# A two-layer fp32 trunk on one core: residual update moved into the next normalisation loop, half of its products on GpSimd, and four smaller reorderings

## The chip, the core and the metric

The kernel runs on one core of a Trainium2 chip. Its engines are TensorE (PE in the profile, its weight loads PEld), VectorE (DVE), ScalarE (ACT), GpSimd (POOL) and SyncE (SP, whose queue issues most of the DMAs). The metric is the device time of one execution in microseconds.

## The reference

Two layers of a diffusion trunk work on 640 tokens (128 context, 512 latent). Each layer is two sandwich-normalised sub-layers with modulation:

```python
h = rmsnorm(x, pre_mix_g) * (1 + sc1) + sh1
x = x + g1 * rmsnorm(token_mixing(h), post_mix_g)
h = rmsnorm(x, pre_ffn_g) * (1 + sc2) + sh2
up = depthwise_conv(h @ ffn_up)                 # 3 taps, 2 x 2816 columns
x = x + g2 * rmsnorm((silu(gate) * val) @ ffn_down, post_ffn_g)
# sh, sc, g = split(silu(c) @ ada_w + ada_b), for each layer and token group
```

Token mixing is one wide input projection, four branches (attention, a depthwise convolution, gated spatial mixing, pooling), sigmoid gates, a merge and an output projection.

## The kernel before

Activations lie with features on the 128 partitions and 644 token columns (640 and halo) along the free axis, in chunks of 128 features: x, yb (the sub-layer's output with its gain, not yet divided by its rms) and h have 8 chunks, the feed-forward `act` 22. Every product is fp32 made of three passes: both operands are split in a high and a low part, and PE runs high*high, high*low (activations) and low*high (weights). Weight blocks of 128x512 come by DMAs of SP's queue into 4 slots; POOL splits each into `w_hi` (L470) and `w_lo` (L472), PE uses them, ACT copies results out of PSUM, DVE does most of the elementwise work. PSUM is used as 4 sets of two banks; counting semaphores `set_full`, `set_empty`, `w_split`, `w_used` pass them round. Each engine runs its own program, a loop over the two layers, so the order on each engine is the order in which the code is written.

A layer's stages: head (`next_mod`, `next_h`: the first h), p1 (input projection), the branches, merge, out, gap2 (`output_norms`, then x is updated and h is made again), up, down, and tail (`output_norms`, x is updated). What the change touches:

- `update_x(c)` (L1401, L1403): yb = yb * inv_rms, x = x + yb, two DVE instructions of 128x644 for each chunk. In gap2 three updates stand ahead of `next_h` and five within it; in tail all eight stand at the end of the layer's loop body.
- `next_h` (L1423, L1433): for each chunk DVE makes `hx` = x * scale * inverse rms, ACT rounds `h_hi`, DVE makes `h_lo`. PE's first group of a stage starts when h_lo of chunk 0 is there.
- At the start of a layer SP requests two rounds of p1's weights, waits on `layer_free`, and requests `par` (gains and biases) and `tables`. POOL waits on the same semaphore, clears `conv_x` and splits weights. In the first layer ACT gives `layer_free` after the head's modulation.
- up: 11 steps of 4 sets; a half step of two sets is called an item here (items 0 to 21; item 2i + q is half q of step i). For an item PE runs two products of 8 feature chunks, ACT copies the two sets into `up_x` (L1234), DVE runs the three taps (L1793, L1798), ACT a tanh, DVE the gate (L1805, L1808). The two sets of an item come free for item + 2 when ACT has copied them. Meanwhile DVE sums "trios" of modulation columns over chunks (`ada`: L1377 twice, L1379 14 times, 128x384); PE adds each trio over partitions with 6 one-column matmuls (L572) ahead of a product, and waits for the trio there.
- down: 2 passes over the 22 chunks of `act`, a chunk is 24 matmuls over all 4 sets; ACT and DVE make the high and low part of a chunk (`hi_part` L1255, `lo_part` L1815) before PE needs it. Between the passes ACT evacuates the 4 sets (`outputs`), and DVE's `add_square`, `cross` and `add_products` (L1307, L1360, L1365, L1367) add up the statistics of the first four output chunks. Chunks are numbered on through both passes, 0 to 43.

## Time and profile before

| | us |
|---|---|
| median of 3 runs | 2651.12 (2649.63 to 2651.96) |
| profiled execution, its own time | 2648.95 |
| its span from the first to the last instruction | 2647.1 |
| PE busy | 2404.7 (91%) |
| DVE busy | 1807.2 (68%) |
| POOL busy | 1332.7 (50%) |
| ACT busy | 555.8 (21%) |

The profile is one execution. Busy shares are averages over stages that wait for different engines, so what one edit is worth is read from the stretch that it touches. In the timeline a row gives the start, the duration, the engine, the line, the operation with its tiles, the count of merged instructions and, in brackets, how long the engine stood idle before and what ended that.

### The profile page before, as it was taken

Reading aid. Unit: us, or ns where it says so; the run is one execution under the profiler, and the core shown is the slowest. Engines: PE = TensorE matmul, PEld = TensorE weight load, DVE = VectorE, ACT = ScalarE, POOL = GpSimd, SP = SyncE. Lnnn points to the kernel's source line nnn. Section 1 sums busy time; section 2 is a strip of 40 time slices with the busy share of each in tenths; the row PEclk is TensorE's granted clock in tenths of the full one; section 3 lists DMA queues with packets and bytes.
Section 4 is the critical chain, followed back from the end, with each engine's and each line's share of the span. In section 5 each row is a group of like instructions: output and inputs, shape, how many; then the busy total and the mean of one; then the engine's idle time right before and its main releaser. Section 6 shows DMA issues by size and latency. Waiting matters only on the chain.

```text
span 2647.1 us, 44389 instructions
## 1 busy us (share of the span) xinstructions
PE 2404.7 (91%) x14854; PEld 2228.2 (84%) x14854; DVE 1807.2 (68%) x2357; ACT 555.8 (21%) x989; POOL 1332.7 (50%) x1240
## 2 busy tenths in 40 slices
PE   5897989999997999999959888899999799999996
PEld 5894548999986999999959744699999689999986
DVE  5558765554489898976573786555436888989566
ACT  1203442111121111123211144410111211111232
POOL 2458314555553656565435761065555445656551
PEclk9998999999997999999969989899999799999997
DMA  5210002333321323322212101033332223323221
...
DMA packets 100491, 212.04 MB, mean 80 GB/s; under 512 B 10208, under 2 KB 17824, under 8 KB 100384
## 3 DMA queue, kind: packets, MB, share of 16 engines
...
q8 instruction: 59, 0.97, 0.2%
q14 instruction: 48, 0.39, 0.1%
...
## 4 chain that ended last, share of the span: by engine, by line
PE 55%; DVE 17%; DVEq 16%; issue 6%; ACT 5%; POOLq 1%; DMA 1%; ACTq 0%; POOL 0%; SPq 0%
PE ps L539 31%; PE ps L883 9%; DVEq L1795 4%; PE ps L559 4%; DVEq L1382 3%; PE ps L755 3%; DVE ada_part L1379 3%; DVEq L1801 3%; DVE up_y L1793 2%; PE ps L701 2%; DVE x L1403 1%; PE ps L572 1%; ACT up_x L1234 1%; DVE yb L1401 1%; PE ps L744 1%
## 5 line engine op out<-in xcount | busy, mean ns | idle before, releaser
L470 POOL TENSOR_SCALAR w_hi<-w_raw 128x512 fp32r<-128x512 f32 x552 | 378.7, 686 | 1107.9 <-PE ps L539 237.5
L472 POOL TENSOR_TENSOR w_lo<-w_raw,w_hi 128x512 fp32r<-128x512 f32 x552 | 769.8, 1395 | 81.4 <-issue 1.4
L539 PE MATMUL ps<-h_hi,w_hi 128*128 128x322 f32 x2688 | 627.5, 315 | 5.3 <-POOL w_lo L472 5.3
L539 PE MATMUL ps<-h_lo,w_hi 128*128 128x322 f32 x2688 | 623.6, 313 | 0.0
L539 PE MATMUL ps<-h_hi,w_lo 128*128 128x322 f32 x2688 | 620.3, 312 | 0.0
L539 PEld LDWEIGHTS ps<-h_hi,w_hi 128*128 128x128 f32 x2688 | 455.5, 191 | 8.7 <-POOL w_lo L472 7.4
L539 PEld LDWEIGHTS ps<-h_lo,w_hi 128*128 128x128 f32 x2688 | 458.2, 191 | 0.0
L539 PEld LDWEIGHTS ps<-h_hi,w_lo 128*128 128x128 f32 x2688 | 458.2, 191 | 0.0
L1379 DVE SCALAR_TENSOR_TENSOR ada_part<-ada_raw,cond,ada_part 128x384 f32<-128x384 f32 x448 | 342.2, 805 | 17.1
L1798 DVE SCALAR_TENSOR_TENSOR up_y<-up_x,par,up_y 128x644 f32<-128x644 f32 x176 | 216.0, 1267 | 13.9 <-issue 12.7
L1815 DVE TENSOR_TENSOR a_lo<-act,a_hi 128x644 fp32r<-128x644 f32 x84 | 130.0, 1549 | 116.1 <-ACT a_hi L1255 113.7
L883 PE MATMUL ps<-a_hi,w_hi 128*128 128x322 f32 x640 | 150.7, 317 | 19.8 <-DVE a_lo L1815 16.3
L1735 DVE SCALAR_TENSOR_TENSOR mtmp<-gate_t,ps 128x644 f32<-128x644 f32 x48 | 39.4, 821 | 173.1 <-ACT gate_t L1181 131.7
L883 PE MATMUL ps<-a_hi,w_lo 128*128 128x322 f32 x640 | 149.5, 316 | 0.0
L883 PE MATMUL ps<-a_lo,w_hi 128*128 128x322 f32 x640 | 149.3, 315 | 0.0
L1241 ACT ACTIVATE up_t<-up_y 128x644 f32<-128x644 f32 x44 | 32.7, 743 | 473.3 <-DVE up_y L1798 473.3
L883 PEld LDWEIGHTS ps<-a_hi,w_hi 128*128 128x128 f32 x640 | 109.0, 193 | 25.2 <-DVE a_lo L1815 18.2
L1181 ACT ACTIVATE gate_t<-ps,half_gate 128x644 f32<-128x644 f32 x64 | 51.2, 800 | 341.0 <-PE ps L539 337.5
L559 PE MATMUL ps<-h_hi,w_hi 128*128 128x322 f32 x256 | 63.5, 331 | 58.5 <-DVE h_lo L1433 58.5
L507 POOL TENSOR_TENSOR conv_acc<-conv_acc,conv_tmp 128x655 f32<-128x655 f32 x60 | 105.9, 1765 | 8.8 <-issue 0.2
L883 PEld LDWEIGHTS ps<-a_hi,w_lo 128*128 128x128 f32 x640 | 109.9, 193 | 0.0
L883 PEld LDWEIGHTS ps<-a_lo,w_hi 128*128 128x128 f32 x640 | 109.6, 193 | 0.0
...
## 6 DMA issues: line engine op xcount, KB each, us to landing
...
```

What stands on the lines that cost most here:

```text
L470: pool.tensor_scalar(w_hi[:, s, 0:n * P], raw, 1.0, 0.0, ALU.mult, ALU.add)
L472: pool.tensor_tensor(w_lo[:, s, 0:n * P], raw, w_hi[:, s, 0:n * P], ALU.subtract).then_inc(w_split[s], 1)
L507: pool.tensor_tensor(conv_acc[:, 0, 0:CLEN], conv_acc[:, 0, 0:CLEN], dst, ALU.add)
L539: last = pe.matmul(ps[:, 2 * s + j, 0:HALF], w, a[:, j * HALF:(j + 1) * HALF], start=(k == 0 and i == 0), stop=(k == total - 1 and i == 2))
L559: last = pe.matmul(ps[:, 2 * s + j, 0:HALF], w, a[:, j * HALF:(j + 1) * HALF], start=(k == 0 and i == 0), stop=(k == DC - 1 and i == 2))
L755: pe.matmul(ps[0:V_HEAD, 7, :], v_pair[:, b, vs], probs_t[:, b, :], start=(b == 0), stop=(b == 4))
L883: last = pe.matmul(ps[:, 2 * s + j, 0:HALF], w, a[:, j * HALF:(j + 1) * HALF], start=(start and i == 0), stop=(stop and i == 2))
L1379: last = dv.scalar_tensor_tensor(out=acc[:, g, 0:n, :], in0=w, scalar=cond[:, k, g:g + 1], in1=acc[:, g, 0:n, :], op0=ALU.mult, op1=ALU.add)
L1382: dv.drain()
L1795: dv.drain()
L1798: last = dv.scalar_tensor_tensor(out=up_y[:, j, :], in0=up_x[:, j, 1 + tap:1 + tap + TOK], scalar=col("ffn_dw", v, tap), in1=up_y[:, j, :] ...
L1815: dv.tensor_tensor(a_part_of(n, False), src, a_part_of(n, True), ALU.subtract).then_inc(a_ready, 1)
```

## The change

Five edits come together.

1. x is updated within the `next_h` that follows. `next_h` first updates chunks 0 and 1, then chunk c + 2 inside its loop, at every call: in gap2, and at the head of a layer, where it now does the update that stood at the end of the layer before (for the first layer with zeros in yb and in the inverse rms, which are cleared at the start). The last layer's update stands after the loop. POOL multiplies chunks 4 to 7 by the inverse rms (`scale_outputs`, after it has split the stage's first round of weights), and DVE only adds those.
2. `ada_pre` and `ada_pre_part` lie at other addresses, and x is requested after the second part of `ada_pre` instead of the third.
3. `par` is requested ahead of p1's weights on a semaphore of its own, `tables` after p1's first round; `layer_free` is given at the start for the first layer; POOL neither waits for it nor clears `conv_x`, which DVE does after `next_h`.
4. Middle of down: the last two chunks of the first pass run set by set (`last_chunks`), and chunks 22 and 23 have buffers of their own, so that ACT and DVE make their parts ahead of the evacuation; each later `lo_part` stands one place earlier among the statistics.
5. up: the trios after the first stand before DVE's items 4, 7, 10, 13, 16, 19 instead of 3, 6, 9, 12, 15, 18, and PE uses them at the second product of items 2, 8, 14 and 20 and at the first of items 6, 12 and 18, instead of at the first product of items 2, 5, 8, 11, 14, 17 and 20.

```diff
+POOL_SCALES = range(DC // 2, DC)
@@ SP
-            sp.wait_ge(ada_pre_loaded[2], 16)
+            sp.wait_ge(ada_pre_loaded[1], 16)
...
-                load_linear(L, "p1", 0, 2)
+                sp.wait_ge(par_free, L + 1)
+                sp.dma_start(par[:, :], params_in[bass.ds(L, 1)].rearrange("a p n -> (a p) n")).then_inc(par_loaded, 16)
+                load_linear(L, "p1", 0, 1)
                 sp.wait_ge(layer_free, L + 1)
-                sp.dma_start(par[:, :], params_in[bass.ds(L, 1)].rearrange("a p n -> (a p) n")).then_inc(par_loaded, 16)
...
+                load_linear(L, "p1", 1, 1)
@@ POOL
+            def scale_outputs(n_inv):
+
+                pool.wait_ge(inv_ready, n_inv)
+                for c in POOL_SCALES:
+                    pool.tensor_tensor(yb[:, c, :], yb[:, c, :], inv_rms[:, :], ALU.mult).then_inc(yb_scaled, 1)
...
-                pool.wait_ge(layer_free, L + 1)
-                pool.sem_inc(pool_steps, 1)
-                pool.memset(conv_x[:, :, :], 0.0).then_inc(halo_zero, 1)
-                split_linear(L, "p1", P1_BLOCKS // SLOTS)
+                split_linear(L, "p1", 1)
+                scale_outputs(L * NINV + 1)
+                split_linear(L, "p1", P1_BLOCKS // SLOTS, 1)
...
-                split_linear(L, "up", UP_BLOCKS // SLOTS)
+                split_linear(L, "up", 1)
+                scale_outputs(L * NINV + 3)
+                split_linear(L, "up", UP_BLOCKS // SLOTS, 1)
@@ PE, up
-                    up_step(r * 3 + 1, late_trio(L, 2) + r * 2, 0)
-                    up_step(r * 3 + 2, late_trio(L, 3) + r * 2, 2)
-                    up_step(r * 3 + 3)
-                up_step(10, late_trio(L, 8), 0)
+                    up_step(r * 3 + 1, late_trio(L, 2) + r * 2, 1)
+                    up_step(r * 3 + 2)
+                    up_step(r * 3 + 3, late_trio(L, 3) + r * 2, 0)
+                up_step(10, late_trio(L, 8), 1)
@@ PE, down
+                def last_chunks(q, first):
+                    end = (q + 1) * FFC - 1
+                    for s in range(4):
+                        for n in range(first, end + 1):
...
-                        for k in range(LAST4, FFC):
-                            down_chunk(q, c0 + k, (c0 + k) // SLOTS, (c0 + k) % SLOTS, k % 2, False, k == FFC - 1)
...
+                        for k in (LAST4, LAST4 + 1):
+                            down_chunk(q, k, k // SLOTS, k % SLOTS, k, False, False)
+                        last_chunks(0, LAST4 + 2)
@@ ACT, down
                 hi_part(FFC, 0)
+                hi_part(FFC + 1, 1)
                 ac.wait_ge(gain_ready, 2 * L + 2)
                 outputs(0)
-                hi_part(FFC + 1, 1)
                 for k in range(2, 2 + SLOTS):
+                    hi_part(FFC + k, k)
                     square_of_scaled(k - 2, down_sq2, L * 2 * DC + DC + k - 2)
-                    hi_part(FFC + k, k)
@@ DVE
-            def update_x(c):
-
-                dv.tensor_tensor(yb[:, c, :], yb[:, c, :], inv_rms[:, :], ALU.mult)
-                dv.drain()
+            def update_x(c, n_scaled):
+
+                if c in POOL_SCALES:
+                    dv.wait_ge(yb_scaled, n_scaled + c - POOL_SCALES[0] + 1)
+                else:
+                    dv.tensor_tensor(yb[:, c, :], yb[:, c, :], inv_rms[:, :], ALU.mult)
+                    dv.drain()
                 return dv.tensor_tensor(x[:, c, :], x[:, c, :], yb[:, c, :], ALU.add)
...
+                dv.wait_ge(inv_ready, n_inv - 1)
+                update_x(0, n_scaled)
+                dv.drain()
+                update_x(1, n_scaled)
+                dv.drain()
                 dv.wait_ge(inv_ready, n_inv)
...
-                    if c + 1 in updates:
-                        update_x(c + 1)
+                    if c + 2 < DC:
+                        update_x(c + 2, n_scaled)
...
-                    up_step(r * 3 + 1, trio=late_trio(L, 3) + r * 2, before=1)
-                    up_step(r * 3 + 2)
-                    up_step(r * 3 + 3, trio=late_trio(L, 4) + r * 2)
+                    up_step(r * 3 + 1)
+                    up_step(r * 3 + 2, trio=late_trio(L, 3) + r * 2)
+                    up_step(r * 3 + 3, trio=late_trio(L, 4) + r * 2, before=1)
...
-                dv.wait_ge(inv_ready, L * NINV + 4)
-                for c in range(DC):
-                    update_x(c).then_inc(x_new, 1)
-                    dv.drain()
+            dv.wait_ge(inv_ready, DEPTH * NINV + 1)
+            for c in range(DC):
+                update_x(c, DEPTH * 2 * len(POOL_SCALES)).then_inc(x_new, 1)
+                dv.drain()
```

First place: DVE in gap2, from the first update to the first h_lo that PE waits for (the file's line numbers differ between the two kernels; sq_sum is the inverse rms's tile). Before:

```order
L1401 TENSOR_TENSOR yb<-yb,sq_sum 128x644 [waits inv_ready]
L1403 TENSOR_TENSOR x<-x,yb 128x644
L1401 TENSOR_TENSOR yb<-yb,sq_sum 128x644
L1403 TENSOR_TENSOR x<-x,yb 128x644
L1401 TENSOR_TENSOR yb<-yb,sq_sum 128x644
L1403 TENSOR_TENSOR x<-x,yb 128x644
L1423 SCALAR_TENSOR_TENSOR hx_up<-x,mod_a,inv_up 128x128 [waits inv_ready]
L1423 SCALAR_TENSOR_TENSOR hx_up<-x,mod_a,inv_up 128x512
L1423 SCALAR_TENSOR_TENSOR hx_up<-x,mod_a,inv_up 128x128
L1423 SCALAR_TENSOR_TENSOR hx_up<-x,mod_a,inv_up 128x512
L1431 ISA
L1433 SCALAR_TENSOR_TENSOR h_lo<-hx_up,mod_b,h_hi 128x128 [waits hi_ready]
```

Of the change, from the wait for the second inverse rms (two updates stand ahead of it) to the first chunk that POOL scales:

```order
L1451 SCALAR_TENSOR_TENSOR hx_up<-x,mod_a,inv_up 128x128 [waits inv_ready]
L1451 SCALAR_TENSOR_TENSOR hx_up<-x,mod_a,inv_up 128x512
L1423 TENSOR_TENSOR yb<-yb,sq_sum 128x644
L1425 TENSOR_TENSOR x<-x,yb 128x644
L1451 SCALAR_TENSOR_TENSOR hx_up<-x,mod_a,inv_up 128x128
L1451 SCALAR_TENSOR_TENSOR hx_up<-x,mod_a,inv_up 128x512
L1423 TENSOR_TENSOR yb<-yb,sq_sum 128x644
L1425 TENSOR_TENSOR x<-x,yb 128x644
L1459 ISA
L1461 SCALAR_TENSOR_TENSOR h_lo<-hx_up,mod_b,h_hi 128x128 [waits hi_ready]
```

Four updates instead of three now stand ahead of the first h_lo; the later ones are one addition each.

Second place: PE where the second step of up begins, the trio's six matmuls and the product behind them. Before:

```order
L568 ISA [waits set_empty0]
L572 MATMUL ps<-const,ada_part 128x1 [waits ada_summed]
L572 MATMUL ps<-const,ada_part 128x1 x5
L531 ISA
L539 MATMUL ps<-h_hi,w_hi 128x322 [waits w_split0]
```

Of the change, after the whole first product of that step:

```order
L553 MATMUL ps<-h_hi,w_lo 128x322 x2
L874 REGISTER_ALU
L582 ISA [waits set_empty1]
L586 MATMUL ps<-const,ada_part 128x1 [waits ada_summed]
L586 MATMUL ps<-const,ada_part 128x1 x5
L553 MATMUL ps<-h_hi,w_hi 128x322 [waits w_split2]
```

The wait for the trio moved from the first set's product to the second's.

Third place: DVE between the passes of down, from the last `add_square` on. Before:

```order
L1307 TENSOR_TENSOR sq_sum<-sq_sum,sq 128x644 [waits sq_ready]
L1815 TENSOR_TENSOR a_lo<-act,a_hi 128x644 [waits a_part]
L1360 TENSOR_TENSOR down_xy<-x,yb 128x644 [waits yb_ready]
L1365 TENSOR_TENSOR down_xy_sum<-down_xy_sum,down_xy 128x644
L1367 TENSOR_TENSOR down_sq_sum<-down_sq_sum,down_sq_103 128x644 [waits sq2_ready]
```

Of the change, from the parts of chunks 22 and 23 on:

```order
L1842 TENSOR_TENSOR b_lo<-act,b_hi 128x644 [waits a_part]
L1840 REGISTER_ALU
L1842 TENSOR_TENSOR b_lo<-act,b_hi 128x644 [waits a_part]
```

Before, the low part after the last `add_square` is that of chunk 23; in the change both chunk 22's and chunk 23's stand ahead of the four `add_square`, and the low part behind them is chunk 24's.

## Rows read from the trace of the kernel before

**Rows 1.** The page, one of the costliest groups: PE's first groups that wait for h.

```profile
L559 PE MATMUL ps<-h_hi,w_hi 128*128 128x322 f32 x256 | 63.5, 331 | 58.5 <-DVE h_lo L1433 58.5
```

**Rows 2.** Timeline, head of the first layer, several engines.

```profile
47.28 1.54 POOL L489 TENSOR_TENSOR sq_sum<-sq_sum,sq 128x644 f32<-128x644 f32 x1 [0.16 <-issue]
...
58.17 0.20 ACT L995 ACTIVATE mod<-ps 128x32 f32<-128x32 f32 x1 [11.97 <-PE ps L628]
...
74.74 0.18 DVE L1497 TENSOR_SCALAR half_gate<-par 128x32 f32<-128x32 f32 x1 [19.63 <-DMA tables<-in_tables_dram]
...
78.74 0.91 PE L559 MATMUL ps<-h_hi,w_hi 128*128 128x322 f32 x2 [18.27 <-DVE h_lo L1433]
```

**Rows 3.** Timeline, end of the first layer to the second's first matmul, DVE and PE.

```profile
1341.80 0.82 DVE L1325 TENSOR_TENSOR diag_next<-const,small 128x640 f32<-128x640 f32 x1
...
1356.22 0.83 DVE L1403 TENSOR_TENSOR x<-x,yb 128x644 f32<-128x644 f32 x1
...
1361.23 0.18 DVE L1497 TENSOR_SCALAR half_gate<-par 128x32 f32<-128x32 f32 x1 [4.19 <-issue]
...
1365.24 0.91 PE L559 MATMUL ps<-h_hi,w_hi 128*128 128x322 f32 x2 [20.06 <-DVE h_lo L1433]
```

**Rows 4.** Timeline, gap2 of the first layer, ACT, PE, POOL and DVE.

```profile
797.92 0.77 ACT L943 ACTIVATE sq_sum<-ps 128x128 f32<-128x128 f32 x2 [12.73 <-PE ps L592]
...
808.67 0.88 PE L559 MATMUL ps<-h_hi,w_hi 128*128 128x322 f32 x2 [6.04 <-DVE h_lo L1433]
...
819.66 1.76 DVE L1403 TENSOR_TENSOR x<-x,yb 128x644 f32<-128x644 f32 x1
...
836.25 1.01 DVE L1433 SCALAR_TENSOR_TENSOR h_lo<-hx_up,mod_b,h_hi 128x128 fp32r<-128x128 f32 x2 [0.17 <-ACT h_hi L954]
```

**Rows 5.** Timeline, up of the first layer: PE at the first trio, DVE's trios and items.

```profile
837.82 1.13 DVE L1377 TENSOR_SCALAR ada_part<-ada_raw,cond 128x384 f32<-128x384 f32 x2 [0.17 <-issue]
...
848.79 1.14 DVE L1793 TENSOR_SCALAR up_y<-up_x,par 128x644 f32<-128x644 f32 x2
...
848.93 2.72 PE L572 MATMUL ps<-const,ada_part 128*128 128x1 f32 x12 [4.66 <-DVE ada_part L1379]
...
855.92 2.40 DVE L1793 TENSOR_SCALAR up_y<-up_x,par 128x644 f32<-128x644 f32 x2
...
869.70 2.15 DVE L1793 TENSOR_SCALAR up_y<-up_x,par 128x644 f32<-128x644 f32 x2 [3.01 <-ACT up_x L1234]
...
880.12 1.12 DVE L1377 TENSOR_SCALAR ada_part<-ada_raw,cond 128x384 f32<-128x384 f32 x2
...
892.90 1.13 DVE L1793 TENSOR_SCALAR up_y<-up_x,par 128x644 f32<-128x644 f32 x2
...
901.17 2.41 DVE L1793 TENSOR_SCALAR up_y<-up_x,par 128x644 f32<-128x644 f32 x2
...
913.94 2.56 DVE L1793 TENSOR_SCALAR up_y<-up_x,par 128x644 f32<-128x644 f32 x2 [0.64 <-ACT up_x L1234]
...
925.51 1.12 DVE L1377 TENSOR_SCALAR ada_part<-ada_raw,cond 128x384 f32<-128x384 f32 x2
```

**Rows 6.** Windows: length, PE busy, PEld, DVE, ACT, POOL, granted clock, DMA.

```profile
852.00:870.00 18.00, 18.00 (x107) 18.00 (x106) 13.05 (x13) 4.34 (x7) 10.78 (x10) 0.85 0.39 131
870.00:1153.00 283.00, 279.66 (x1887) 278.33 (x1886) 253.82 (x250) 41.39 (x66) 168.68 (x151) 1.00 0.32 98
1164.00:1222.90 58.90, 58.77 (x384) 58.50 (x384) 29.34 (x24) 11.15 (x15) 29.96 (x30) 0.97 0.23 67
```

**Rows 7.** Timeline, PE at the first chunks of down, first layer.

```profile
1153.11 0.56 PE L883 MATMUL ps<-a_hi,w_hi 128*128 128x322 f32 x2 [0.76 <-DVE a_lo L1815]
...
1164.11 0.64 PE L883 MATMUL ps<-a_hi,w_hi 128*128 128x322 f32 x2 [3.62 <-DVE a_lo L1815]
```

**Rows 8.** Timeline, middle of down, first layer: DVE's low part of chunk 27 and PE at it.

```profile
1262.55 0.83 DVE L1815 TENSOR_TENSOR a_lo<-act,a_hi 128x644 fp32r<-128x644 f32 x1 [0.16 <-issue]
...
1263.44 0.57 PE L883 MATMUL ps<-a_hi,w_hi 128*128 128x322 f32 x2 [0.91 <-DVE a_lo L1815]
```

More of the change, by code:

```diff
@@ L1258, in _ @@
                 with ac.Fori(0, 3) as r:
-                    up_step(r * 3 + 1, keep="rows", row=r * (2 * ADA_TRIO) + ADA_TRIO, trio=(1, r * 2))
-                    up_step(r * 3 + 2, keep="rows", row=r * (2 * ADA_TRIO) + 2 * ADA_TRIO, trio=(2, r * 2), ada_set=2)
-                    up_step(r * 3 + 3)
-                up_step(FFC // 2 - 1, last=True, keep="last")
+                    up_step(r * 3 + 1, keep="rows", row=r * (2 * ADA_TRIO) + ADA_TRIO, trio=(1, r * 2), ada_set=1)
+                    up_step(r * 3 + 2)
+                    up_step(r * 3 + 3, keep="rows", row=r * (2 * ADA_TRIO) + 2 * ADA_TRIO, trio=(2, r * 2))
+                up_step(FFC // 2 - 1, last=True, keep="last", ada_set=1)
                 def outputs(q):
@@ L1504, in _ @@
                 dv.memset(pool_x[:, :], 0.0)
+                dv.memset(conv_x[:, :, :], 0.0)
                 dv.drain()
@@ L1767, in _ @@
                 output_norms(L, "gap2", diag_up, diag_up2)
[L1768 to L1772 removed]
+                next_h(L, L * 2 + 1, L * NINV + 4, hx_up, inv_up)
                 for j in range(4):
```

101 lines of the change are left out of this document (52 added, 49 removed).

## The prediction

> **What bounds the kernel now.** The list of waits comes first, because the change touches no product: it can only shorten or lengthen PE's standing still, and PE is busy 91% of the span. The page has one such wait next to the change: the first groups that start on a fresh h wait 58.5 us for DVE's h_lo [rows 1]. Then the timeline of each of these places, to see what DVE did meanwhile. In the first layer PE waits 18.27 for h and DVE itself had waited 19.63, for the DMA of the tables [rows 2]. At the second layer's head PE waits 20.06: DVE first does eight updates of x, 14.43 from 1342.62 to 1357.05, so 1.80 each, then stands 4.19 with no release that the profile shows as its loop returns, and needs 4.0 from `half_gate` to the first h_lo [rows 3]. In gap2 PE waits 6.04 [rows 4]. In up I read DVE and PE side by side: PE waits 4.66 for the first trio, and later trios end a few us before PE asks, since DVE is nearly full there (253.8 of 283) [rows 5, 6]. The windows also price a fallen clock: 1887 rows of matmul pairs in 279.66 are 0.148 each at granted clock 1.00, so the 107 of the window after the 4.66 wait (clock 0.85) took 2.1 too long, and the 384 after a wait of 3.62 (clock 0.97) took 1.9 too long [rows 6, 7].
>
> **Head of the first layer.** The tables no longer stand ahead of `half_gate`; modulation is ready at 58.37 [rows 2]. From there 4.0 as before, and four updates ahead of the first h_lo (two before the loop, two within it): 58.4 + 0.2 + 4.0 + 4 x 1.80 = 69.8, against 78.74. Their data are zeros, their time is not. POOL now multiplies four chunks; one such instruction took 1.54 [rows 2], which is 1.9 of DVE's 0.83, so the sharing itself saves DVE 0.9 a chunk and needs POOL 1.5. What an instruction of DVE pays when it meets one of POOL with two operands is seen in gap2: an addition of 0.83 took 1.76 [rows 4], 0.93 more. Four products, one meeting each: 3.7, so 73.5, a gain of **5.2**. Bounds: 8.9 if POOL is done earlier; a loss of 1.0 if its four weight splits, which no longer wait, also hold DVE's sums of `ada_pre` by a product's 1.54 each. I take one meeting each, the row nearest by size. The clearing of yb (eight chunks, about 6.6 at DVE's 0.83 a chunk) is before DVE has its first columns, that of `conv_x` (about 1.8 by the same scale) behind DVE's last h_lo, when PE has a group of its own to run; without that cover they would cost these times. The new addresses and the earlier request of x shift POOL's sums of squares, which end before DVE's do; nothing.
>
> The Trainium skill, "SBUF — State Buffer", section "SBUF: two separate sides", speaks against this part: the port pair that VectorE and GpSimd share is an exclusive lock, kept for the whole instruction by whoever started first, and a VectorE instruction with two operands in SBUF needs it. By that rule each product holds DVE up to its full 1.54, not 0.93, and this head gains 2.7 instead of 5.2; the 1.76 above is in keeping with a blocked instruction, but does not show how much of POOL's instruction it waited out.
>
> **Head of the second layer.** From `diag_next` at 1342.62: 4.19 for the loop's return, which I leave, 4.0, four updates 7.2: PE at 1358.0 instead of 1365.24 [rows 3], a gain of **7.2**. POOL's products (6.2) start with the inverse rms and fall into the 4.19; if DVE still meets all four, 3.5 is left; if the 4.19 shrinks away, 11.4. The remaining updates are inside PE's first group, 0.9 each for chunks 4 to 7; a chunk then needs about 3 of DVE and 24 pairs of 0.148, 3.6, of PE, so PE sets the pace.
>
> **gap2.** One more update and the four meetings ahead of the first h_lo: 808.67 + 1.8 + 3.7 = 814.2. Behind it four additions replace four pairs, 3.6 less, so the last h_lo stays near 837.3 [rows 4], the first trio ends at 849 as before, and PE's first group ends near 844.8 (192 pairs, 28.5, and 2.1 of low clock). This costs nothing as long as the first trio's later place, next, hides it.
>
> **up.** An item is 96 pairs, 14.2 of PE; a trio on PE is 1.4 (2.72 at half clock) [rows 5]. DVE needs 7.1 for item 0, 10.8 for item 1, 10.4 for item 2, 8.3 for an item straight after a trio, 11.6 or 12.1 for others; the first trio took 11.0, with PE standing, the next 12.8 [rows 5]. The first trio is now asked for at the second product of item 2, so the 4.66 goes. DVE: 849, then items 0 to 3 to 889, trio to 901.7, item 4 to 910.0, item 5 to 922.1, item 6 (11.85, the middle) to 933.9, and the trio before item 7, which PE waits for, 11.9 (middle of 11.0 and 12.8): 945.8. PE asks for it at 844.8 + 6.5 x 14.2 + 2 x 1.4 = 939.9: it waits 6. This is the point of the part: from there on a trio stands alternately 2 and 1.5 items ahead of its use, and the half item that is missing is 7.1 of PE. The next round from that release: PE has item 8 full 8.5 later and item 9 at 22.7; DVE does item 8 from 9.5 to 21.1, waits, item 9 from 23.7 to 35.3, trio to 48.1, items 10 to 12 to 80.3, trio to 92.2; PE asks at 88.0 and waits 4.2. Two rounds: 1130.2, and 1.4 + 7.1 + 14.2 + 0.2 to the first chunk of down: 1153.1, where it is now [rows 7]. So three new waits give back what the first one's removal brought. Each is long enough to lower the clock as the 3.62 one did, 1.9: **a loss of 5.7 a layer**, 11.4 in both. Bounds: a gain of 10 (trios of 11.0, items of 10.4, no fall of the clock), a loss of 15 (12.8, 12.1, and 2.1 + 1.4 after each wait, as after the 4.66).
>
> **Middle of down.** PE reached chunk 28 at 1263.44 + 24 x 0.148 = 1267.0, because the low part of chunk 27 came last of DVE's chain, at 1263.38 [rows 8]. That place is now chunk 28's, chunk 23's low part having gone ahead of the statistics; set 0 is full about 0.5 earlier, as chunks 20 and 21 share it back to back. Chunk 28 at 1262.8: a gain of **4.2**, twice. PE alone would be there before: the last set is emptied near 1242, and chunks 22 to 27 are 21.4. Bounds: 2.3 with one more fall of the clock (1.9), 6.1 if the chain loses as much of its meetings with POOL.
>
> **End.** Eight updates, 14.4, become four pairs and four additions, 10.8; with four meetings 14.5: **0.1** lost; bounds a gain of 3.6 and a loss of 2.6 (four times 1.54).
>
> **The sum** is made against the profiled execution's 2648.95 (span 2647.1 and 1.85 around it), 2.17 under the median: -5.2 - 7.2 + 11.4 - 8.4 + 0.1 = -9.3, so 2639.65 there and **2641.8** by the median. What this measurement can tell from no change is about 0.2%, 5.3 us.
>
> **Rivals.** (1) The trios in up come in time: for it speaks that DVE has 29 of 283 idle there; against, the count above. Then up gains 4.66 and 1.4 a layer instead of losing 5.7; the other terms are -20.7, so -32.8: 2618.3. (2) The waits in up cost about 10 a layer, trios at 12.8 throughout and the clock falling: -0.7, 2650.4. (3) Slower: the odd trio's wait, at the second product of the steps that hold items 8, 14 and 20, costs its upper bound of 15 a layer; from 13 a layer on it eats all the rest and 5.3 more. +9.3: 2660.4. For it speaks that DVE is already the pace of up. (4) The middle of down gains nothing, since DVE's statistics still end last there: -0.9, 2650.2. (5) Each of POOL's products holds DVE its whole 1.54, at the first head and at the end: 2.5 more at both, 2646.8; the row of 1.76 beside 0.83 bears it out in part. It is what the Trainium skill's rule in "SBUF — State Buffer", section "SBUF: two separate sides", would do here.
>
> **Chances.** Forecast 0.49 (its own range 2634 to 2645.8), rivals 0.10, 0.15, 0.11, 0.09, 0.06. Faster by over 0.2%: 0.49 + 0.10 = 0.59; within: 0.15 + 0.09 + 0.06 = 0.30; slower: 0.11. Eight in ten lie from 2624 (the better half of the first rival left out) to 2655 (half of the third, and what lies beyond, left out).
>
> **What would show it.** `half_gate` no longer behind a DMA and PE's first group near 73 in layer 1; 15 to 16 us, not 22.6, from `diag_next` to PE's first matmul of layer 2; in gap2 a first h_lo later by 5 to 6 and a first trio that PE does not wait for; then three waits of 3 to 6 for `ada_part` in each up, at the second product, with a granted clock below 1 behind them; in down, chunk 28 reached 4 sooner counted from chunk 20. The prediction is wrong if these three waits are missing or much longer, or if DVE's updates beside POOL's products stretch well over 1.76.

## The result, and the profile after

The changed kernel takes 2663.48 us, the median of 5 runs (2656.17 to 2666.64), against 2651.12 for the kernel before on the same chip: the ratio is 1.0042, with a 95% interval from 1.003 to 1.0054. It became 12.4 slower where the prediction had it 9.3 faster.

| | us |
|---|---|
| profiled execution, its own time | 2660.77 |
| its span | 2658.8 |
| PE busy | 2403.0 (90%) |
| DVE busy | 1829.8 (69%) |
| POOL busy | 1368.9 (51%) |
| ACT busy | 554.5 (21%) |

The list of waits of PE after: engine and tile, releaser, then total, times and the longest.

```profile
PE ps L573 <- DVE h_lo L1461: 43.7, 4, 13.2
...
PE ps L586 <- DVE ada_part L1398: 27.8, 8, 5.0
```

The waits for h fell from the 58.5 of [rows 1] to 43.7, while PE's waits just ahead of them, for `diag_up` and `diag_next` (the inverse rms as DVE lays it out for PE), rose from 6.9 to 17.0. Those for `ada_part`, the trios of up, rose from 10.3 to 27.8, and the list alone doesn't tell whether the one pays for the other. So I cut the spans at events of PE that every kernel has: its first matmul of a stage, and its sums over partitions at the tail. "Head 1" runs from the start to layer 1's first matmul, "gap2 + up" from gap2's sums on PE to the first matmul of down, "down" from there to the tail's sums, "head 2" from those to layer 2's first matmul, "end" from layer 2's tail to the end. "Rest" is p1 to gap2 in both layers; a single layer's share of it, from the second product group on, lay between 677.6 and 684.3 over all kernels, whatever was changed, so differences of some us there mean nothing. All kernels of this study are in the table, since the experiments are read in it.

| profiled span, us | head 1 | gap2 + up | down | head 2 | gap2 + up | down | end | rest | span |
|---|---|---|---|---|---|---|---|---|---|
| before | 78.7 | 364.1 | 175.2 | 36.9 | 364.3 | 175.4 | 28.5 | 1423.9 | 2647.1 |
| after | 75.3 | 377.7 | 173.9 | 28.1 | 378.3 | 170.6 | 29.8 | 1425.1 | 2658.8 |
| e1 trios back | 75.3 | 364.5 | 180.0 | 28.1 | 364.7 | 176.8 | 29.2 | 1426.4 | 2644.9 |
| e2 trios alone | 78.7 | 375.8 | 171.9 | 36.9 | 377.6 | 171.9 | 28.6 | 1426.5 | 2667.8 |
| e3 all products on DVE | 70.5 | 378.4 | 174.0 | 26.5 | 378.4 | 170.6 | 28.0 | 1433.9 | 2660.2 |
| e4 down alone | 78.8 | 364.1 | 173.9 | 36.9 | 362.5 | 176.5 | 28.1 | 1422.0 | 2642.8 |
| e5 trios 2.5 ahead | 75.4 | 366.5 | 178.9 | 28.1 | 366.7 | 175.4 | 29.3 | 1428.9 | 2649.2 |
| e6 trios back, DVE | 70.6 | 364.2 | 177.4 | 26.1 | 364.3 | 174.0 | 28.1 | 1426.3 | 2631.0 |
| e7 edits 1 to 3 | 75.5 | 364.7 | 179.1 | 28.1 | 364.8 | 175.7 | 30.2 | 1428.6 | 2646.7 |
| e8 PE kept busy | 75.0 | 373.1 | 175.5 | 27.8 | 373.1 | 172.2 | 29.4 | 1422.3 | 2648.2 |
| e9 used half an item later | 75.1 | 364.2 | 175.7 | 27.8 | 364.2 | 172.3 | 30.2 | 1424.2 | 2633.6 |
| e10 edits 2 and 3 | 64.5 | 364.5 | 178.8 | 33.7 | 364.5 | 175.5 | 28.7 | 1418.9 | 2629.0 |
| e11 = e10 + first trio later | 64.7 | 365.0 | 177.0 | 33.7 | 364.3 | 175.3 | 28.7 | 1425.2 | 2634.0 |
| e12 = e9 without edit 4 | 75.2 | 363.8 | 176.7 | 28.1 | 363.8 | 173.4 | 30.2 | 1422.1 | 2633.1 |

Gap2 with up lost 13.6 and 14.1 in the two layers, and that is more than the whole result. Here is up of the first layer in the timeline of after, DVE and PE; it answers to [rows 5].

```profile
852.04 1.14 DVE L1820 TENSOR_SCALAR up_y<-up_x,par 128x644 f32<-128x644 f32 x2
...
869.81 2.40 DVE L1820 TENSOR_SCALAR up_y<-up_x,par 128x644 f32<-128x644 f32 x2
...
881.84 2.40 DVE L1820 TENSOR_SCALAR up_y<-up_x,par 128x644 f32<-128x644 f32 x2
...
893.88 1.12 DVE L1396 TENSOR_SCALAR ada_part<-ada_raw,cond 128x384 f32<-128x384 f32 x2
...
938.91 1.12 DVE L1396 TENSOR_SCALAR ada_part<-ada_raw,cond 128x384 f32<-128x384 f32 x2
940.12 11.56 DVE L1398 SCALAR_TENSOR_TENSOR ada_part<-ada_raw,cond,ada_part 128x384 f32<-128x384 f32 x14
951.59 1.14 DVE L1820 TENSOR_SCALAR up_y<-up_x,par 128x644 f32<-128x644 f32 x2
951.73 2.72 PE L586 MATMUL ps<-const,ada_part 128*128 128x1 f32 x12 [4.99 <-DVE ada_part L1398]
...
964.86 1.32 DVE L1820 TENSOR_SCALAR up_y<-up_x,par 128x644 f32<-128x644 f32 x2 [4.58 <-ACT up_x L1253]
...
978.37 2.13 DVE L1820 TENSOR_SCALAR up_y<-up_x,par 128x644 f32<-128x644 f32 x2 [3.84 <-ACT up_x L1253]
...
988.79 1.12 DVE L1396 TENSOR_SCALAR ada_part<-ada_raw,cond 128x384 f32<-128x384 f32 x2
...
1034.19 1.12 DVE L1396 TENSOR_SCALAR ada_part<-ada_raw,cond 128x384 f32<-128x384 f32 x2
...
1047.21 2.72 PE L586 MATMUL ps<-const,ada_part 128*128 128x1 f32 x12 [4.13 <-DVE ada_part L1398]
...
1142.87 2.69 PE L586 MATMUL ps<-const,ada_part 128*128 128x1 f32 x12 [4.22 <-DVE ada_part L1398]
```

Windows of the same kernel around the first of these waits: the wait, what follows it, and the rest of the round (length; PE, PEld, DVE, ACT, POOL busy; granted clock; DMA).

```profile
946.00:951.70 5.70, 0.74 (x5) 0.47 (x4) 5.40 (x10) 0.00 (x0) 0.37 (x1) 0.89 0.16 46
951.70:958.00 6.30, 6.27 (x28) 6.27 (x29) 5.14 (x7) 1.37 (x2) 0.70 (x2) 0.56 0.00 1
958.00:1042.00 84.00, 84.00 (x568) 84.00 (x567) 67.24 (x66) 11.27 (x18) 53.19 (x47) 1.00 0.35 109
```

PE stands while DVE sums the trio. Then it runs 6.3 us at a granted clock of 0.56, near the lower of its two levels, and its products come late to DVE, which had been the late one and now stands 4.58 and 3.84 itself. After that PE is never idle for 84 us, until the next trio. DVE's list of waits has the same over the whole span, before and after:

```profile
DVE up_y L1793 <- ACT up_x L1234: 7.4, 4, 3.2
DVE up_y L1820 <- ACT up_x L1253: 46.7, 16, 5.0
```

DVE stands 39.3 longer for up's products, and gap2 with up is 27.7 longer in both layers together.

In gap2 the reader sees what POOL's products do to DVE (timeline of after, POOL, DVE and PE; [rows 4] before).

```profile
800.35 7.23 POOL L491 TENSOR_TENSOR yb<-yb,sq_sum 128x644 f32<-128x644 f32 x4 [13.27 <-ACT sq_sum L962]
800.59 1.35 DVE L1340 SCALAR_TENSOR_TENSOR small<-small 128x5 f32<-128x5 f32 x1
802.01 2.08 DVE L1344 TENSOR_TENSOR diag_up<-const,small 128x640 f32<-128x640 f32 x1
804.02 2.17 DVE L1423 TENSOR_TENSOR yb<-yb,sq_sum 128x644 f32<-128x644 f32 x1
806.26 2.01 DVE L1425 TENSOR_TENSOR x<-x,yb 128x644 f32<-128x644 f32 x1
...
817.00 0.87 PE L573 MATMUL ps<-h_hi,w_hi 128*128 128x322 f32 x2 [10.35 <-DVE h_lo L1461]
```

While POOL makes its four products in 7.23 us, DVE finishes four instructions. Free of POOL they take 0.17, 0.82, 0.83 and 0.83 in the same trace; here they add up to 7.61, 4.96 more. The first is a step on 5 columns, which pays as much as an update: when it is held, DVE is still making the second inverse rms, and has no work on x yet.

### The profile page after: what moved, and what is told of

The parts are those of the page before. It is cut to its first block, busy times and chain, and to the rows that moved or that the text cites. A ratio compares the mean times of both kernels' runs of the same rounds, so it can differ in the third digit from the quotient of the medians.

```text
span 2658.8 us, 44434 instructions
## 1 busy us (share of the span) xinstructions
PE 2403.0 (90%) x14854; PEld 2228.6 (84%) x14854; DVE 1829.8 (69%) x2357; ACT 554.5 (21%) x989; POOL 1368.9 (51%) x1258
## 4 chain that ended last, share of the span: by engine, by line
PE 59%; DVE 18%; DVEq 13%; issue 4%; ACT 4%; DMA 1%; POOL 0%; ACTq 0%; SPq 0%; POOLq 0%
PE ps L553 39%; PE ps L897 8%; DVEq L1401 3%; PE ps L769 3%; DVE ada_part L1398 3%; DVEq L1822 2%; PE ps L573 2%; PE ps L586 2%; PE ps L715 2%; DVE x L1425 1%; DVEq L1828 1%; PE ps L745 1%; DVEq L1465 1%; DVEq L1387 1%; PE ps L758 1%
## 5 line engine op out<-in xcount | busy, mean ns | idle before, releaser
L476 POOL TENSOR_SCALAR w_hi<-w_raw 128x512 fp32r<-128x512 f32 x552 | 384.1, 696 | 1076.2 <-PE ps L553 248.9
L553 PE MATMUL ps<-h_hi,w_hi 128*128 128x322 f32 x2688 | 628.6, 315 | 6.7 <-POOL w_lo L478 6.7
L1825 DVE SCALAR_TENSOR_TENSOR up_y<-up_x,par,up_y 128x644 f32<-128x644 f32 x176 | 202.8, 1193 | 14.0 <-issue 12.7
L897 PE MATMUL ps<-a_hi,w_hi 128*128 128x322 f32 x576 | 133.0, 312 | 11.4 <-DVE a_lo L1842 11.1
L897 PE MATMUL ps<-a_hi,w_lo 128*128 128x322 f32 x576 | 132.5, 311 | 0.0
L897 PE MATMUL ps<-a_lo,w_hi 128*128 128x322 f32 x576 | 132.3, 311 | 0.0
L1820 DVE TENSOR_SCALAR up_y<-up_x,par 128x644 f32<-128x644 f32 x88 | 82.2, 975 | 46.7 <-ACT up_x L1253 46.7
L897 PEld LDWEIGHTS ps<-a_hi,w_hi 128*128 128x128 f32 x576 | 96.6, 189 | 14.6 <-DVE a_lo L1842 14.6
L745 PE MATMUL ps<-k_t,q_rot 96*128 96x512 f32 x128 | 82.9, 734 | 27.5 <-DVEq L1667 19.2
L1274 ACT ACTIVATE a_hi<-act 128x644 fp32r (+1 forms) x80 | 59.1, 741 | 211.1 <-PE ps L897 210.5
## 6 DMA issues: line engine op xcount, KB each, us to landing
x<-in_x_dram SPq DMA_DIRECT2D x8, 322.0 KB, 12.7
```

The source lines that it names most:

```text
L476: pool.tensor_scalar(w_hi[:, s, 0:n * P], raw, 1.0, 0.0, ALU.mult, ALU.add)
L553: last = pe.matmul(ps[:, 2 * s + j, 0:HALF], w, a[:, j * HALF:(j + 1) * HALF], start=(k == 0 and i == 0), stop=(k == total - 1 and i == 2))
L745: pe.matmul(ps[:, 2 * s, :], q_rot[0:QK, hd, j * P:(j + 1) * P], k_t[0:QK, hd, 0:DEC_SEQ], start=True, stop=True)
L897: last = pe.matmul(ps[:, 2 * s + j, 0:HALF], w, a[:, j * HALF:(j + 1) * HALF], start=(start and i == 0), stop=(stop and i == 2))
L1820: dv.tensor_scalar(up_y[:, j, :], up_x[:, j, 2:2 + TOK], col("ffn_dw", v, 1), col("ffn_dw_b", v), ALU.mult, ALU.add)
L1825: last = dv.scalar_tensor_tensor(out=up_y[:, j, :], in0=up_x[:, j, 1 + tap:1 + tap + TOK], scalar=col("ffn_dw", v, tap), in1=up_y[:, j, :] ...
```

## The experiments

Twelve kernels ran, each against the kernel before on the same chip. My theory after the result: the trios at the second product (edit 5) cost 13 to 14 a layer, because each odd trio is asked for half an item too early, by PE's clock as much as by the wait. The rivals: gap2's later h (edit 1) pushes DVE, and so all of up; or POOL's products do.

**e1_trios_back**: after, with edit 5 undone on PE, ACT and DVE.

```diff
-                    up_step(r * 3 + 1, late_trio(L, 2) + r * 2, 1)
-                    up_step(r * 3 + 2)
-                    up_step(r * 3 + 3, late_trio(L, 3) + r * 2, 0)
-                up_step(10, late_trio(L, 8), 1)
+                    up_step(r * 3 + 1, late_trio(L, 2) + r * 2, 0)
+                    up_step(r * 3 + 2, late_trio(L, 3) + r * 2, 2)
+                    up_step(r * 3 + 3)
+                up_step(10, late_trio(L, 8), 0)
```

> The changed kernel with edit 5 alone undone (trios at their old places in up). Theory T (the trios that stand half an item short cost the time): the three waits of 4.1 to 5.0 in each up and the low clock behind them go, the first trio's wait of about 5 comes back; up from its first group to the first chunk of down takes about 346 instead of 351.5, and 13 less counted from the end of gap2's sums; about 12 us under the kernel before, 2639. Rival S (GpSimd's products, which hold DVE, cost the time): undoing the trios brings only the fallen clock back, some 3 a layer; still 4 to 6 slower than before, 2656.

Measured: 2643.34, ratio 0.9972 (0.9961 to 0.9983). Gap2 with up takes 364.5 and 364.7, as before the change, though h comes 6.7 later: that delay is hidden behind the old trios, as the prediction's gap2 part said. The rival on gap2 falls.

**e2_trios_alone**: the kernel before, with edit 5 alone (the reverse of e1's edit).

> The kernel before with edit 5 alone. T: three new waits of 3 to 5 in each up as in the changed kernel, rounds of 95 us for six items instead of 90.8; about 12 a layer slower, 2675. S: the waits in up come from DVE being late out of gap2, which is not so here; within 5 of before.

Measured: 2667.38, ratio 1.0068 (1.0055 to 1.0081). Timeline of PE in its first layer, the first odd trio and the third chunk of down:

```profile
950.33 2.72 PE L572 MATMUL ps<-const,ada_part 128*128 128x1 f32 x12 [5.02 <-DVE ada_part L1379]
...
1176.21 0.56 PE L883 MATMUL ps<-a_hi,w_hi 128*128 128x322 f32 x2 [1.84 <-DVE a_lo L1815]
```

The wait is 5.02 where after has 4.99, without any of the other edits. Edit 5 does its harm by itself, +11.7 and +13.3 in gap2 with up. Part comes back: down is 3.3 and 3.5 shorter, because PE comes later to chunk 2 and waits 1.84 there instead of 3.62 [rows 7]. So the run lost 19 in all and not the expected 12 a layer.

**e3_dve_scales**: after, with all products on DVE again.

```diff
-POOL_SCALES = range(DC // 2, DC)
+POOL_SCALES = range(0)
...
-                scale_outputs(L * NINV + 1)
...
-                scale_outputs(L * NINV + 3)
...
-            scale_outputs(DEPTH * NINV + 1)
```

> The changed kernel with all eight products on DVE, none on GpSimd, all else as changed. T: gap2's first matmul comes about 5 earlier after the sums (21.5 instead of 26.4), but DVE has four more products inside the loop (3.6), so the first trio ends about where it did and up keeps its three waits; the end is 3.6 longer or, without the meetings, 1.5 longer; 0 to 5 less than the changed kernel, 2658 to 2663. S: gap2's 6.7 a layer and most of the heads' loss come back, 13 or more less than the changed kernel, at or under before.

Measured: 2661.08, ratio 1.0039 (1.0026 to 1.0052), as after's within both intervals. The heads are 4.8 and 1.5 shorter without POOL, and the first group of a layer behind them 2.9 and 3.8 longer, since DVE now does eight products there. The sharing gains and loses alike; the rival on POOL falls as a cause of the loss.

**e4_down_alone**: the kernel before, with edit 4 alone.

```diff
+                        for k in (LAST4, LAST4 + 1):
+                            down_chunk(q, k, k // SLOTS, k % SLOTS, k, False, False)
+                        last_chunks(0, LAST4 + 2)
...
+                hi_part(FFC + 1, 1)
...
-                hi_part(FFC + 1, 1)
...
+                lo_part(FFC + 1, 1)
...
+                    lo_part(FFC + k, k)
...
-                    lo_part(FFC + k, k)
```

> The kernel before with edit 4 alone (middle of down). By the changed kernel's trace PE goes from chunk 20 to chunk 28 in 35.4 instead of 36.75, so 1.3 a layer: 2648.5, hardly measurable. By the prediction's own step 4.2 a layer: 2642.7. A third reading, that the 4.7 a layer by which down is shorter in the changed kernel is all due to this edit, gives 2641.7 with the shortening at the start of down too (chunk 2 waiting 1.85 instead of 3.62).

Measured: 2647.27, ratio 0.9999 (0.999 to 1.0007). Down changes by -1.3 and +1.0, so the forecast 4.2 a layer isn't there. PE at chunk 28 of the first layer still waits for DVE's low part:

```profile
1265.91 0.57 PE L884 MATMUL ps<-a_hi,w_hi 128*128 128x322 f32 x2 [1.53 <-DVE a_lo L1821]
```

**e5_trios_25**: after, with DVE's trios at their old places and each used 2.5 items after it stands, at second products.

```diff
-                    up_step(r * 3 + 2)
-                    up_step(r * 3 + 3, late_trio(L, 3) + r * 2, 0)
+                    up_step(r * 3 + 2, late_trio(L, 3) + r * 2, 3)
+                    up_step(r * 3 + 3)
...
-                    up_step(r * 3 + 1)
-                    up_step(r * 3 + 2, trio=late_trio(L, 3) + r * 2)
-                    up_step(r * 3 + 3, trio=late_trio(L, 4) + r * 2, before=1)
+                    up_step(r * 3 + 1, trio=late_trio(L, 3) + r * 2, before=1)
+                    up_step(r * 3 + 2)
+                    up_step(r * 3 + 3, trio=late_trio(L, 4) + r * 2)
```

> The changed kernel with edit 5 replaced: DVE sums the trios at the places of the kernel before (items 3, 6, ..., 18), PE uses each at the second product (items 2, 5, 8, ..., 20), so every trio stands 2.5 items ahead of its use. Theory T (the missing half item costs the time): no wait of PE for a trio anywhere in up, the first included; from up's first matmul to down 335 or a little less, instead of 351.5 changed and 338.1 with the old places; 2636 to 2641. Rival C (the second product is the wrong place for a trio, whatever its lead): waits as in the changed kernel, 2655 or more.

Measured: 2646.41, ratio 0.9992 (0.9982 to 1.0001). No trio is waited for, but up takes 340.1, not the 335 hoped for. PE stands elsewhere instead:

```profile
902.54 0.57 PE L553 MATMUL ps<-h_hi,w_hi 128*128 128x322 f32 x2 [4.07 <-POOL w_lo L478]
```

POOL had waited 10.43 for ACT before that split, and ACT for DVE's taps. DVE sets the pace of up, and a lead of one trio more only moves the place where PE finds that out. The miss is mine: I had taken PE's pace as the floor.

**e6_back_dve**: e1 and e3 together.

> The changed kernel with edit 5 undone and all eight products on DVE. Theory T: with trios at the old places PE waits for the first trio anyway, so the 5 us that gap2 saves are lost again in DVE's four more products; within 4 of the run with edit 5 undone alone (2643). Rival S (sharing costs time that the odd trios' waits had covered up): 8 or more below it.

Measured: 2639.02, ratio 0.9963 (0.9949 to 0.9978), beside e1's 0.9972: sharing the products brings nothing here either.

**e7_edits123**: after with edits 4 and 5 undone.

> The changed kernel with edits 4 and 5 undone: the update in the next loop, the shared products and the early requests alone. If edit 4 is worth nothing, as its run alone says: within 2 of the run with edit 5 undone, some 7 under before. If edit 4 costs 1.3 a layer beside the rest, as the stretch of down says in the run with edit 5 undone (176.7 without the longer tail, against 175.3 before): 2 to 3 less than that run.

Measured: 2646.03, ratio 0.999 (0.998 to 1.0). Head 1 gains 3.2 and head 2 8.9, but layer 1's down is 3.9 longer and the end 1.7. Neither reading of the expectation came out: by the ratios this run is 4.8 slower than e1, with intervals that just overlap, though its down is 0.9 and 1.1 shorter.

**e8_busy**: after, with 16 matmuls of 128 columns of ones, into columns that nobody reads, ahead of each trio at a second product (in the timeline each counts twice, as the trio's six do). PE then works where it would stand; the trio comes no sooner.

```diff
+                            if j == 1:
+                                for _ in range(16):
+                                    pe.matmul(ps[:, 2 * j + 1, HALF:HALF + P], ones[:, :], ones[:, :], start=True, stop=True)
```

> The changed kernel with 16 matmuls of 128 columns of ones, into columns that nobody reads, ahead of each trio that PE takes at its second product, so that PE is busy for some 3 of the 4 to 5 us that it waits there. Theory T with the clock's price (a third of a layer's loss in up is the low clock and the slow trio behind each wait): the granted clock stays near 1.00 behind the trio, its six matmuls take 1.4 instead of 2.7, a round of six items takes 92 to 93 instead of 95.5, 6 to 9 less a layer: 2645 to 2651. If the wait alone is the price: the same as the changed kernel, or slower by what the matmuls overrun.

Measured: 2652.24, ratio 1.001 (1.0001 to 1.002). Timeline of PE at the first and second odd trio, then the windows behind them:

```profile
942.86 3.73 PE L878 MATMUL ps<-const 128*128 128x128 f32 x32
948.02 1.50 PE L586 MATMUL ps<-const,ada_part 128*128 128x1 f32 x12 [1.43 <-DVE ada_part L1401]
...
1042.50 1.50 PE L586 MATMUL ps<-const,ada_part 128*128 128x1 f32 x12 [0.57 <-DVE ada_part L1401]
```

```profile
948.00:954.00 6.00, 5.98 (x33) 5.99 (x34) 4.84 (x7) 1.22 (x2) 0.56 (x1) 0.72 0.01 1
1042.50:1047.00 4.50, 4.50 (x33) 4.50 (x34) 4.14 (x6) 0.00 (x0) 0.00 (x0) 1.00 0.00 0
```

With work that does nothing, up is 4.7 and 5.3 shorter, less than the 6 to 9 expected. In the window behind a remaining wait of 0.57 the clock is 1.00, behind 1.43 it is 0.72, behind 4.99 it was 0.56; the trio takes 1.50, not 2.72. So about 5 of the 14 a layer are the clock's. The other 9 are there with the clock mostly up (8.9 and 8.8 over before): the products still come late, and DVE still stands 33.8 for them over the span.

**e9_half_later**: after, with the odd trios used at the next item's first product, half an item later.

```diff
-                    up_step(r * 3 + 1, late_trio(L, 2) + r * 2, 1)
+                    up_step(r * 3 + 1, late_trio(L, 2) + r * 2, 2)
...
-                up_step(10, late_trio(L, 8), 1)
+                up_step(10, late_trio(L, 8), 2)
...
-                    up_step(r * 3 + 1, keep="rows", row=r * (2 * ADA_TRIO) + ADA_TRIO, trio=(1, r * 2), ada_set=1)
+                    up_step(r * 3 + 1, keep="rows", row=r * (2 * ADA_TRIO) + ADA_TRIO, trio=(1, r * 2), ada_set=2)
...
-                up_step(FFC // 2 - 1, last=True, keep="last", ada_set=1)
+                up_step(FFC // 2 - 1, last=True, keep="last", ada_set=2)
```

> The changed kernel with one number moved: PE takes the trios of items 2, 8, 14 and 20 at the first product of the next item (3, 9, 15, 21), half an item, 7.1 us, later; DVE's places stay those of the change. Theory T (the missing half item): the waits of 5.0, 4.1 and 4.2 fall within 7.1 and vanish, up takes 338 to 341 instead of 351.5; 2640 to 2646, under before. If DVE's places, and not the half item, cost the time: up stays at 348 or more, 2655 or more.

Measured: 2635.63, ratio 0.9955 (0.9941 to 0.9969), 0.9% below after. Its list of waits and its windows of up in the first layer:

```profile
PE ps L586 <- DVE ada_part L1398: 1.3, 2, 0.8
```

```profile
846.00:1148.00 302.00, 296.43 (x1990) 294.71 (x1989) 269.55 (x268) 44.02 (x71) 177.40 (x158) 0.99 0.31 99
```

The waits for trios fall from 27.8 to 1.3, the granted clock over up is 0.99, and gap2 with up is back at 364.2; DVE stands 3.3 for up's products instead of 46.7. This decides it: the order on DVE is still that of the change, and only the use on PE moved by half an item.

**e10_early**: the kernel before, with edits 2 and 3 alone.

```diff
-            sp.wait_ge(ada_pre_loaded[2], 16)
+            sp.wait_ge(ada_pre_loaded[1], 16)
...
+                sp.wait_ge(par_free, L + 1)
+                sp.dma_start(par[:, :], params_in[bass.ds(L, 1)].rearrange("a p n -> (a p) n")).then_inc(par_loaded, 16)
+                load_linear(L, "p1", 0, 1)
...
-                pool.wait_ge(layer_free, L + 1)
-                pool.sem_inc(pool_steps, 1)
-                pool.memset(conv_x[:, :, :], 0.0).then_inc(halo_zero, 1)
...
+                dv.memset(conv_x[:, :, :], 0.0)
```

> The kernel before with edits 2 and 3 alone: parameters, tables and x requested earlier, POOL no longer waiting for the layer to be free, the clearing on DVE; no update of x moved, no product shared, down and up as before. The reading of the changed kernel's trace that the first layer's head lost most of its gain to four updates of zeros and their meetings with POOL: here the first matmul of layer 1 comes at 63 to 66 instead of 75.3 (before 78.7), its first group as long as before; layer 2's head as before; 12 to 15 under before, about 2635. If the requests are not what held the head: 75 or more there, and at most 4 gained.

Measured: 2635.0, ratio 0.996 (0.9947 to 0.9974). Its timeline at the head of layer 1 and at the tail's sums:

```profile
57.82 1.25 DVE L1498 TENSOR_SCALAR half_gate<-par 128x32 f32<-128x32 f32 x1
...
64.47 0.91 PE L559 MATMUL ps<-h_hi,w_hi 128*128 128x322 f32 x2 [4.01 <-DVE h_lo L1433]
...
1316.82 2.27 PE L583 MATMUL ps<-const,sq_sum 128*128 128x1 f32 x10 [6.76 <-DVEq L1308]
```

Two small edits on requests bring the first matmul 14.3 sooner than [rows 2], and all five together only 3.4. The difference, 10.8, is edit 1: updates of x by zeros ahead of the first h, 6.0 of it DVE's own (e3's 70.5) and 4.8 the meetings with POOL's products.

**e11_early_mixed**: e10, with the odd trios used at the second product of items 2, 8, 14 and 20, and DVE's trios at their old places.

```diff
-                    up_step(r * 3 + 1, late_trio(L, 2) + r * 2, 0)
+                    up_step(r * 3 + 1, late_trio(L, 2) + r * 2, 1)
...
-                up_step(10, late_trio(L, 8), 0)
+                up_step(10, late_trio(L, 8), 1)
```

> Edits 2 and 3 alone, and PE takes the trios of items 2, 8, 14 and 20 at the second product instead of the first, DVE's places as before (leads of 2.5 and 2 items in turn). The first trio's wait of 4.7 and the low clock behind it should go; DVE sets the pace behind, so 0 to 4 a layer: 0 to 8 less than edits 2 and 3 alone.

Measured: 2635.52, ratio 0.9958 (0.9944 to 0.9971). Removing the first trio's wait of 4.66 brings nothing over e10: gap2 with up is 365.0 and 364.3 where e10 has 364.5 twice. PE waits 20.3 for POOL's `w_lo` instead of 5.7: the place of the wait moved.

**e12_half_no4**: e9 with edit 4 undone.

> The changed kernel with the odd trios used half an item later and edit 4 undone. What edit 4 is worth beside the others is open: alone it gave nothing (0.9999), with edit 5 undone the runs with and without it stood at 0.9972 and 0.9990. If it is worth nothing: within 2 us of the same kernel with edit 4 (2635.6, ratio 0.9955). If it gains the 4.2 a layer that was predicted: 8 more than that, 2644, ratio 0.9987.

Measured: 2638.85, ratio 0.9968 (0.9957 to 0.9979), beside e9's 0.9955. The intervals overlap. By the medians edit 4 is worth 3.4 us in both layers together (0.13% of 2650), in the stretch of down 0.9 and 1.1; what it is worth stays open. No run shows the prediction's 8.4 for it.

## Why the prediction was wrong

**The step that failed is the part on up**, in its count of DVE's time: the sum that let the first chunk of down come at 1153.1, "where it is now". The waits themselves were foreseen: the first trio's 4.66 went, and three waits at the second product of items 8, 14 and 20 came, 4.99, 4.13 and 4.22 where 6, 4.2 and 4.2 were forecast. What they cost was not: 13.6 and 14.1 a layer instead of 5.7. Rival 3, which ended slower from 13 a layer on, is what happened. By the prediction's own steps, in the first layer: the first matmul of down was forecast at 1153.1, with 5.7 for the clock to be added, and came at 1168.34, of which 1.6 was there at gap2's sums already. That leaves 13.6.

- The first odd trio was ready at 951.6 instead of 945.8, 4.3 later without those 1.6. The first trio ended at 852.04 and not 849, so 1.4 later without the 1.6; items 2 and 3 took 12.0 each instead of 10.4 and 11.6; and the odd trio took 12.68 (938.91 to 951.59), though I had counted 11.9 because PE stands meanwhile.
- The rounds took 95.5 (951.73 to 1047.21) and 95.7, instead of 92.2 each: 6.7 more. I had started a round with the trio's 1.4 and PE at full clock. In fact the trio itself ran at the lower clock, 2.72, and the products behind it 6.3 us long at 0.56, so item 8 reached DVE 13.3 after the release and not 9.5. Of that delay 1.9 was left when DVE was through with item 9, at 37.2 and not 35.3; I count it to the clock. From there to the next release it took 58.3 instead of 56.9: the three items 0.4 more, the odd trio 12.9 instead of 11.9. That is 1.4, DVE's. The second round divides in the same way, 2.0 and 1.4.
- From the last release to down it took 25.5 instead of 22.9, 2.6 more: the trio took 2.69, and the clock was 0.54 in the 6.2 us from 1142.8 on.

So the clock cost 6.5 by this count (1.9, 2.0 and 2.6), where three times 1.9 stood in the sum, and e8, whose dummy matmuls took 4.7 and 5.3 a layer away, agrees: that term was about right. The other 7.1 (4.3 and twice 1.4) is DVE's own time, where the sum had nothing. I had taken 10.4 for item 2 from a row behind a stand of DVE, and 11.9 for the odd trios from the middle of 11.0 and 12.8 [rows 5]; with no stand before it item 2 took 12.0, and the odd trios took 12.7 to 12.9 although PE stood beside them. The prediction's upper bound of 15, with 12.8 and 12.1, had these times. And the removal of the first wait, which the first rival priced at 4.66 and 1.4 a layer, is worth nothing where DVE sets the pace (e11).

**Head of the first layer.** Forecast 73.5, measured 75.31:

```profile
59.43 1.52 DVE L1528 TENSOR_SCALAR half_gate<-par 128x32 f32<-128x32 f32 x1
...
61.12 1.36 DVE L1435 SCALAR_TENSOR_TENSOR mod_a<-mod,par 128x16 f32<-128x16 f32 x1
...
62.73 1.93 DVE L1423 TENSOR_TENSOR yb<-yb,sq_sum 128x644 f32<-128x644 f32 x1 [0.16 <-issue]
64.73 2.01 DVE L1425 TENSOR_TENSOR x<-x,yb 128x644 f32<-128x644 f32 x1
...
75.31 0.90 PE L573 MATMUL ps<-h_hi,w_hi 128*128 128x322 f32 x2 [13.24 <-DVE h_lo L1461]
```

`half_gate` began 1.0 later than I took it: POOL's four weight splits, which no longer waited, fell on DVE's small steps towards the rms, of which six took 0.28 to 1.10 instead of 0.17, and the inverse rms's tile was cleared just ahead of them (0.59), so `diag_next` came at 58.68 where it had been at 54.29. And the four meetings with POOL cost 4.8 (1.52, 1.36, 1.93 and 2.01 instead of 0.17, 0.18, 0.83 and 0.83), not 3.7. The gain is 3.4, and 2.1 with the first group, which took 1.4 longer. In the three places with four products (here, gap2 and below) DVE's instructions are stretched by 1.1 to 1.4 each, except for the last one below (0.3), between the 0.93 that I took and the full 1.54 of rival 5. What I had not asked is which instructions meet: `half_gate`, `mod_a` and the small steps towards an rms, 0.17 long, were among them.

The Trainium skill, "SBUF — State Buffer", section "SBUF: two separate sides", says that VectorE and GpSimd lock their shared port pair for a whole instruction. The trace agrees in that each product stretches one instruction of DVE, however short: 0.17 became 1.35 in gap2.

**Head of the second layer.** Timeline of after, POOL, PE and DVE ([rows 3] before):

```profile
1333.81 1.67 POOL L478 TENSOR_TENSOR w_lo<-w_raw,w_hi 128x512 fp32r<-128x512 f32 x1
...
1342.28 2.26 PE L597 MATMUL ps<-const,sq_sum 128*128 128x1 f32 x10 [6.76 <-DVEq L1327]
...
1352.80 6.62 POOL L491 TENSOR_TENSOR yb<-yb,sq_sum 128x644 f32<-128x644 f32 x4 [8.44 <-ACT sq_sum L962]
...
1355.93 2.08 DVE L1344 TENSOR_TENSOR diag_next<-const,small 128x640 f32<-128x640 f32 x1
...
1359.00 0.46 DVE L1528 TENSOR_SCALAR half_gate<-par 128x32 f32<-128x32 f32 x1 [0.98 <-issue]
...
1370.33 0.90 PE L573 MATMUL ps<-h_hi,w_hi 128*128 128x322 f32 x2 [9.76 <-DVE h_lo L1461]
```

From the tail's sums to PE's first matmul it is 28.05 instead of 36.92, a gain of 8.9 where 7.2 was forecast. But the sums themselves come 3.4 later, PE waiting 6.76 there and not 3.40: POOL no longer waits for `layer_free` and splits p1's weights just when DVE adds up the last statistics. e10 shows the same 6.76 without edit 1, and the second layer, which has no split there, doesn't show it. Before, the same splits had met DVE's small steps behind the sums (timeline of before):

```profile
1332.64 1.11 DVE L1317 TENSOR_TENSOR small<-small 128x5 f32<-128x5 f32 x1
```

So edit 3 moved this collision from one side of the sums to the other: in e10, 3.2 of the 8.9 are there without edit 1 (33.7), against the 3.4. Edit 1's own share is 5.6: 7.2 for four updates fewer and 2 or so of DVE's stand as its loop returns (0.98; 3.07 in e10, 4.19 before), less some 4 for POOL's products, which met small steps and `diag_next` and not that stand. That the gain came near the forecast is in part luck. With 1.0 in the first group and the 3.4 the net gain is 4.5. The prediction had named such a collision for the first layer's `ada_pre` and not looked for the splits one layer on.

**gap2.** Forecast 814.2, 817.00 measured, 1.6 of it from before: +6.7, not +5.5. It costs nothing by itself, as forecast (e1, e9); beside edit 5 it costs 1.9 and 0.7 (377.7 and 378.3 against e2's 375.8 and 377.6).

**Middle of down.** Down became 4.7 shorter without the 3.4 of the later sums, and 4.9 in the second layer, near the forecast 4.2, but by luck, for another reason. Timeline of PE after, chunk 2, the last chunk of the first pass and chunks 25 and 28:

```profile
1177.48 0.57 PE L897 MATMUL ps<-a_hi,w_hi 128*128 128x322 f32 x2 [1.85 <-DVE a_lo L1842]
...
1245.21 0.56 PE L916 MATMUL ps<-a_hi,w_hi 128*128 128x322 f32 x2 [2.08 <-DVE a_lo L1842]
...
1262.80 0.57 PE L897 MATMUL ps<-a_hi,w_hi 128*128 128x322 f32 x2 [0.38 <-DVE a_lo L1842]
...
1277.63 0.56 PE L897 MATMUL ps<-a_hi,w_hi 128*128 128x322 f32 x2 [1.53 <-DVE a_lo L1842]
```

The wait at chunk 2 is 1.8 shorter, and the clock behind it 1.00 instead of 0.97, worth 1.9: 3.7 that edit 5 gives back, as e2's 3.3 and 3.5 show. Some 1 is left for edit 4; counted from e1 it is a loss, since with the old trios down is 0.9 and 1.1 longer with edit 4 than without (e1 against e7). The early parts have a price that I had not looked for, 2.08 at the low part of the last chunk of the first pass; and DVE's statistics still end last, with waits at chunks 25 to 28. This part went as rival 4.

**End.** 1.3 longer, forecast 0.1. With all products on DVE it is 0.5 shorter (e3's 28.0), so POOL's cost 1.8 here.

Together, in the spans: -2.1 (first head), -4.5 (second head), +27.7 (gap2 with up), -9.5 (down) and +1.3 (end), and -1.2 in stretches that vary between executions anyway: +11.7, from 2647.1 to 2658.8.

Six versions are faster than both kernels with intervals that exclude no change: e9 (0.9955), e11, e10, e6, e12 and e1 (0.9972). None of them has edit 5 as it stands. What e10 and e7 show together is that the update in the next loop loses more at the first head (11.0) than it saves at the second one (5.6): e10's 64.5 and 33.7, e7's 75.5 and 28.1. A version that skips the updates in the first layer wasn't tried.
